# A four-layer fp32 transformer kernel: the MLA mixer's attention as a row pipeline over head pairs, and two reorderings in the last mixer

## The reference

```python
def _mla_mixer(x, w_in, g_q, g_kv, w_uq, w_ukv, w_o):
    h = x @ w_in
    c_q, c_kv, k_rope = jnp.split(h, [MLA_Q_RANK, MLA_Q_RANK + MLA_KV_RANK], axis=-1)   # 384, 256, 64
    c_q = _rmsnorm(c_q, g_q)
    c_kv = _rmsnorm(c_kv, g_kv)
    q = (c_q @ w_uq).reshape(b, s, MLA_HEADS, MLA_NOPE + MLA_ROPE)      # 8 heads of 128 + 64
    kv = (c_kv @ w_ukv).reshape(b, s, MLA_HEADS, MLA_NOPE + MLA_V)      # 8 heads of 128 + 128
    q_rope = _apply_rope(q_rope, cos[:, None, :], sin[:, None, :])
    k_rope = _apply_rope(k_rope, cos, sin)
    # blocks of 128 queries; chunk-causal mask; softmax over the keys; p @ v
    return o @ w_o

def odd_mixer(x, w_in, forget_b, dw_w, dw_b, cn_g, cn_b, w_out):
    p = x @ w_in
    y_c = forgetting_attention(q, k, v, log_f).reshape(bsz, s, D_C)     # 8 heads of 64
    y_d = conformer_conv(p[..., 3 * D_C + H_C:], dw_w, dw_b, cn_g, cn_b)
    return jnp.concatenate([y_c, y_d], axis=-1) @ w_out
```

## Time and profile before

| | |
|---|---|
| median of 3 runs | 2426.18 us (2425.48 to 2428.16) |
| the profiled execution | 2430.45 us |
| its span in the profile | 2428.7 us |
| TensorE busy | 2341.0 us, 96% |
| DVE, ACT, Pool busy | 753.6, 664.3, 1056.1 us |
| DMA | 213.91 MB, 88 GB/s |

### The profile page before, as it was taken

The page is one execution under the profiler, slowest core; times in us unless marked ns, Lnnn a source line. Parts: engine busy times, 40 slices in busy tenths (PEclk is TensorE's granted clock), DMA queues, the critical chain, the costliest instruction groups (busy, mean ns, idle before and its releaser), DMA issues.

```text
span 2428.7 us, 24625 instructions
## 1 busy us (share of the span) xinstructions
PE 2341.0 (96%) x10347; PEld 1867.6 (77%) x10347; DVE 753.6 (31%) x1434; ACT 664.3 (27%) x889; POOL 1056.1 (43%) x369
## 2 busy tenths in 40 slices
PE   8999999999999989999999999999998998999998
PEld 6666788888777668888878878888876666888887
DVE  6565200002555550000046230010169635000003
ACT  2222322222232322212222222222243463221221
POOL 4213454454323336544445645545431224654443
PEclk9999999999999989999999999999999999999999
DMA  5103222222211113222223222222220112322221
GB/s 198 40 35 121 104 88 104 95 88 95 96 53 44 65 57 122 104 94 97 83 91 108 104 105 102 89 104 78 96 95 27 44 53 87 121 104 95 96 83 56
DMA packets 32366, 213.91 MB, mean 88 GB/s; under 512 B 3584, under 2 KB 4736, under 8 KB 9216
## 3 DMA queue, kind: packets, MB, share of 16 engines
q1 hardware_dynamic: 32256, 212.34, 24.5%
HBM read 210.23 MB, written 2.10 MB: 87 GB/s over the span
## 4 chain that ended last, share of the span: by engine, by line
PE 89%; DVE 8%; ACT 1%; issue 1%; POOL 1%; DMA 0%; SPq 0%; DVEq 0%; ACTq 0%
PE bank L891 17%; PE bank L893 17%; PE bank L892 17%; PE bank L941 9%; PE bank L943 9%; PE bank L942 9%; PE bank L922 3%; DVE bank L1872 2%; PE bank L1172 1%; PE bank L927 1%; PE bank L1074 1%; PE bank L1234 1%; PE bank L1153 1%; PE bank L1279 1%; PE bank L1232 1%
## 5 line engine op out<-in xcount | busy, mean ns | idle before, releaser
L738 POOL TENSOR_TENSOR wlo<-raw,whi 128x2048 fp32r<-128x2048 f32 (+4 forms) x184 | 848.9, 4616 | 534.8 <-ACT whi L420 534.8
L891 PE MATMUL bank<-XH,whi 128*128 128x512 f32 x1832 | 722.4, 394 | 7.3 <-POOL wlo L792 6.2
L893 PE MATMUL bank<-XH,wlo 128*128 128x512 f32 x1832 | 714.9, 390 | 0.0
L892 PE MATMUL bank<-XL,whi 128*128 128x512 f32 x1832 | 714.7, 390 | 0.0
L420 ACT CAST whi<-raw 128x2048 fp32r<-128x2048 f32 (+4 forms) x184 | 350.6, 1909 | 410.3 <-PE bank L941 300.6
L891 PEld LDWEIGHTS bank<-XH,whi 128*128 128x128 f32 x1832 | 344.8, 188 | 97.4 <-issue 20.6
L893 PEld LDWEIGHTS bank<-XH,wlo 128*128 128x128 f32 x1832 | 344.7, 188 | 73.0
L892 PEld LDWEIGHTS bank<-XL,whi 128*128 128x128 f32 x1832 | 345.0, 188 | 69.6
L1571 DVE TENSOR_TENSOR hf<-sil,bank 128x512 f32<-128x512 f32 x88 | 60.5, 687 | 902.4 <-PE bank L893 855.1
L752 POOL TENSOR_TENSOR HL<-hf,HH 128x512 fp32r<-128x512 f32 x88 | 113.9, 1295 | 399.4 <-ACT HH L458 399.4
L941 PE MATMUL bank<-whi,HH 128*128 128x512 f32 x704 | 274.4, 390 | 0.0
(11 more groups left out here) (247 smaller groups left out, 2187.2 us busy)
## 6 DMA issues: line engine op xcount, KB each, us to landing
raw<-w_ffn_gu SPq DMA_DIRECT2D x88, 1024.0 KB, 4.7
raw<-w_ffn_dn SPq DMA_DIRECT2D x40, 1024.0 KB, 4.7
raw<-w_diff_in SPq DMA_DIRECT2D x7, 1536.0 KB, 6.5
GB<-gb SPq DMA_DIRECT2D x8, 1024.0 KB, 7.3
raw<-w_ev_in SPq DMA_DIRECT2D x6, 1024.0 KB, 4.8
raw<-w_od_in SPq DMA_DIRECT2D x4, 1536.0 KB, 6.6
raw<-w_mla_pair SPq DMA_DIRECT2D x4, 1280.0 KB, 6.3
raw<-w_mla_o SPq DMA_DIRECT2D x4, 1024.0 KB, 5.8
```

What stands on the lines that cost most here:

```text
L738: pool.tensor_tensor(wlo[:, off:off + size], raw[:, off:off + size], whi[:, off:off + size].bitcast(F32), ALU.subtract).then_inc(lo_ready, 1)
L891: release(pe.matmul(out, whi[:, off:off + P], xh, start=start, stop=False))
L892: pe.matmul(out, whi[:, off:off + P], xl, start=False, stop=False)
L893: return pe.matmul(out, wlo[:, off:off + P], xh, start=False, stop=stop)
```

## The change

**MLA.** The unit of swapped columns goes, in mla_in and in each pair (a pair's unit falls from 2560 to 2176 columns, eight tiles to seven). Rotation is made from one tile: DVE multiplies each quarter of 32 partitions by the sine and writes it to its neighbouring quarter, four operations, then one with the cosine and the sum. The latents' order is turned: key-value latents and the rotary key in unit 0, query latents in unit 1; pair 0's first eight steps (key and value tiles) come between the latents' groups. The loop is the odd mixer's: s = 0 to 15, both heads per step, normalisation and copies of transposes by ACT, p @ v of the pair before at qb = 1. Outputs are split from PSUM: ACT copies the bank to `XH`, DVE subtracts to `XL`; Pool has no part in it. `mVT` lies now over X, and a second probability buffer `mPT1` over the norm's parameters `GB`, so X is loaded when pair 3 begins and the first `GB` after the last output is split. `out_pair` replaces `out_units` for this mixer.

**Odd mixer.** The diagonals 20 to 30 are written ahead of `keep_conv(1)`. Outputs of pairs 0 and 1 are split from PSUM into `fYH` and `fYL`. ACT splits the last weight units at s = 12 and 14 instead of 13 and 15; its casts of k = 4, 5 come at the end of s = 12 instead of its beginning.

```diff
-STREAM = [("mla_in", (3072, 3072, 1024)), ("mla_pair", (2560,) * 4), ...
+STREAM = [("mla_in", (3072, 3072)), ("mla_pair", (2176,) * 4), ...
-PLACED = {("mla_o", 1): 2048, ("diff_in0", 1): 1536}
+PLACED = {("ffn0_gu", 1): 0, ("diff_in0", 1): 1536}
-MLA_K = (3, 3, 3, 3, 2, 2, 2, 2)
+MLA_K = (2, 2, 2, 2, 3, 3, 3)
+MLA_STEPS = [(t, k) for t in range(7) for k in range(MLA_K[t])]
+MLA_SLOTS = (MLA_STEPS[0:3], MLA_STEPS[3:5], MLA_STEPS[5:8], MLA_STEPS[8:9], MLA_STEPS[9:12], MLA_STEPS[12:13], MLA_STEPS[13:17], [])
@@ SP
-                if norm:
-                    sp.wait_ge(xn_ready, 8 * norm)
+                sp.wait_ge(*((xn_ready, 8 * norm) if norm else (va_free, 16)))
-                if u == 9:
-                    sp.wait_ge(w_used, 7)
+                if u == FIRST_UNIT["mla_o"] + 2:
+                    sp.wait_ge(w_used, FIRST_UNIT["mla_o"])
                     for t in range(NB):
                         sp.dma_start(X[:, t, :], x[t]).then_inc(x_in, 16)
@@ ACT, MLA
+            def mla_high(p):
+                for m in range(2):
+                    vax.add()
+                    act.wait_ge(va_done, vax.at())
+                    act.copy(XH[:, 2 * p + m, :], bank[6 + m][:]).then_inc(oh_ready, 1)
+            for s in range(17):
+                p, qb = divmod(s, 4)
+                if s < 16:
+                    for m in range(2):
+                        exp_row(...)
+                    sums_inverted()
+                    for m in range(2):
+                        scale_row(...)
+                if qb == 0 and s < 16:
+                    vax.add(2)
+                if qb == 1 and p:
+                    mla_high(p - 1)
+                for m in range(2) if s else ():
+                    keep_p(mPT[m], 6 + m, (s - 1) % 4)
+                if qb == 1 and p < 3 or s in (12, 13):
+                    split_w()
+            mla_high(3)
             split_w(2)
@@ ACT, odd mixer
             sigmoid(2)
+            diagonals(range(20, TAPS))
             keep_conv(1, conv_done, 1)
-            diagonals(range(20, TAPS))
             keep_conv(0, dg_used, TAPS)
...
-                if s == 12:
-                    act.wait_ge(tile_free, tiles.at())
-                    act.wait_ge(va_free, lows)
-                    for k in (0, 1):
-                        act.copy(XH[:, k, :], fY[:, k, :]).then_inc(act_hi, 1)
-                    for k in (4, 5):
-                        split_at(XH[:, k, :], fC[:, k - 4, :], swished, k - 3)
...
-                if qb == 1 or s == 15:
+                if qb == 1 and p < 3 or s in (12, 14):
                     split_w()
-                if s == 13:
-                    for k in (6, 7):
+                if s == 12:
+                    act.wait_ge(tile_free, tiles.at())
+                if s in (12, 13):
+                    for k in ((4, 5), (6, 7))[s - 12]:
                         split_at(XH[:, k, :], fC[:, k - 4, :], swished, k - 3)
@@ TensorE, MLA
+            off = begin_unit()
+            pe.wait_ge(latent_lo, 2)
+            mla_steps(off, MLA_STEPS[0:5])
+            mean_squares(5, sq[1], QR)
+            mla_steps(off, MLA_STEPS[5:8])
             spread_root(6)
+            for k in range(3):
+                pe.wait_ge(latent_lo, 3 + k)
+                mla_steps(off, MLA_STEPS[8 + k:9 + k])
+            mla_steps(off, MLA_STEPS[11:])
+            for s in range(16):
+                ...
+                for m in range(2):
+                    claim(4 + m)
+                    pe.matmul(bank[4 + m][:, 0:n], mQN[i][m][:, qb * P:n], mKN[i][m][:, 0:n], start=True, stop=False)
+                ...
+                if qb == 1 and p:
+                    mla_attend(p - 1)
+                if p < 3:
+                    mla_steps(off, MLA_SLOTS[2 * qb])
+                else:
+                    mla_out((0, 2, 4, 5)[qb])
+                for m in range(2) if s else ():
+                    p_transposes(6 + m, mL[(s - 1) % 2][m], (s - 1) % 4 + 1)
+                if p < 3:
+                    mla_steps(off, MLA_SLOTS[2 * qb + 1])
+                elif qb < 2:
+                    mla_out((1, 3)[qb])
+            for m in range(2):
+                p_transposes(6 + m, mL[1][m], NB)
+            mla_attend(3)
+            out_pair(OUT_KS, attended, (mla_late,))      # mla_late: mla_out(6), mla_out(7)
@@ DVE
+            def rope(dst, b):
+                dve.wait_ge(tile_done, tiles.at(1))
+                for q in range(4):
+                    a, o = 32 * q, 32 * (q ^ 1)
+                    dve.tensor_tensor(shift[o:o + 32, :], bank[b][a:a + 32, :], sinT[a:a + 32, :], ALU.mult).then_inc(step, 1)
+                    steps.add()
+                take(lambda: dve.tensor_tensor(dst[:], bank[b][:], cosT, ALU.mult))
+                dve.wait_ge(step, steps.at())
+                dve.wait_ge(tile_free, tiles.at())
+                dve.tensor_tensor(dst[:], dst[:], shift[:], ALU.add).then_inc(rope_ready, 1)
+            latent_tile(3, 0, sq[0], True, False)
+            latent_tile(4, 1, sq[0], False, True)
+            rope(KR, 2)
+            mean_square_root(5, RMS_EPS)
+            from_pe()
+            latents((3, 4), 7)
+            low_latents((3, 4))
+            for j in range(3):
+                latent_tile(j, (3, 0, 1)[j], sq[1], j == 0, j == 2)
+            mean_square_root(5, RMS_EPS)
+            from_pe()
+            latents((0, 1, 2), 6)
+            low_latents((0, 1, 2))
...
-                if qb == 1 and 0 < p < 3:
-                    take_value(lambda: dve.tensor_copy(fY[:, p - 1, :], bank[6][:]))
+                if qb == 1 and p in (1, 2):
+                    ohs.add()
+                    dve.wait_ge(oh_ready, ohs.at())
+                    take_value(lambda: dve.tensor_tensor(fYL[:, p - 1, :], bank[6][:], fYH[:, p - 1, :].bitcast(F32), ALU.subtract))
```

More of the change, by code:

```diff
@@ L181, in build @@
         CL = sb("CL", [P, 5, S], F32R, idle)
+        mVT = [sb(f"mVT{m}", [P, S], F32, idle) for m in range(2)]
         idle.close()
@@ L185, in build @@
         fPT1 = sb("fPT1", [P, NB, S], F32, idle)
+        idle.close()
+        idle = ExitStack()
+        mPT1 = sb("mPT1", [P, NB, S], F32, idle)
         idle.close()
@@ L1195, in _ @@
                 tile((3, 0, 1)[t], [off + (k * 3 + t) * P for k in range(KD)])
+                if t == 0:
+                    mean_squares(5, sq[0], KVR)
                 if t == 1:
-                    mean_squares(5, sq[1], QR)
-            spread_root(6)
-            mean_squares(5, sq[0], KVR)
-            off = begin_unit()
-            claim(2)
-            for k in range(KD):
-                if k == KD // 2:
-                    spread_root(7)
-                ins = product(bank[2][:], off + k * P, XH[:, k, :], XL[:, k, :], k == 0, k == KD - 1)
@@ new lines, in _, with mla_offset, mla_steps @@
+                    spread_root(7)
+            def mla_offset(t, k):
+                return (k * 4 + t) * P if t < 4 else 8 * P + (k * 3 + t - 4) * P
+            def mla_steps(off, slot):
+                steps(off, slot, MLA_K, mla_offset, CH, CL, (2, 3, 0, 1, 2, 3, 0), (3, 3, 3, 3, 0, 0, 0))
+            off = begin_unit()
[3 more added lines that the diff above has]
+            mla_steps(off, MLA_STEPS[5:8])
+            spread_root(6)
@@ L1258, in _, with mla_late @@
-                value_product(ML, mV[i][1], slice(0, P), slice(0, P), 1 if p < 3 else 0)
-            out_steps(off, OUT_MLA[-1])
-            out_units()
+                    mla_steps(off, MLA_SLOTS[2 * qb + 1])
+                elif qb < 2:
+                    mla_out((1, 3)[qb])
+            for m in range(2):
+                p_transposes(6 + m, mL[1][m], NB)
+            mla_attend(3)
+            def mla_late():
+                mla_out(6)
+                mla_out(7)
+            out_pair(OUT_KS, attended, (mla_late,))
@@ new lines, in _ @@
+            for t in range(7):
+                mla_tile(0, t)
+            for s in range(17):
+                p, qb = divmod(s, 4)
+                i, c = p % 2, 2 * (s % 2)
+                for m in range(2) if s < 16 else ():
+                    n = (qb + 1) * P
+                    row_logits(mL[s % 2][m][:, 0:n], 4 + m, n, maskT, MLA_SCALE, negmax[:, c + m:c + m + 1])
+                for m in range(2) if qb == 0 and p < 4 else ():
+                    take_value(lambda: dve.tensor_copy(mV[i][m][:].rearrange("p k d -> p (k d)"), bank[6 + m][:]))
+                if s < 16:
+                    inverse_sums(c)
+                if qb == 1 and p or s == 16:
+                    for m in range(2):
+                        low_value(2 * (p - 1) + m, 6 + m)
+                for t in finished(MLA_SLOTS[2 * qb] + MLA_SLOTS[2 * qb + 1], MLA_K) if p < 3 else ():
+                    mla_tile((p + 1) % 2, t)
```

260 lines of the change are left out of this document (82 added, 178 removed).

## The result

The changed kernel takes 2384.73 us (median of 4 runs, 2384.01 to 2388.51), the kernel before 2426.11 on the same chip: a ratio of 0.9831, 95% interval 0.9814 to 0.9848, 41.4 us less. I had forecast 24.9 us by the profile and 2401 as the median, with 2392 to 2413 as the range. It is faster, as forecast, but by more than the range allows. The profiled execution took 2385.15 (span 2383.4), so by profiled executions the gain is 45.3; the kernel before had been profiled in an execution 4.3 above its median, the changed one in one 0.4 above.

The account below looks back on a forecast made before the run. TensorE, busy 96% of the span, was taken as the bound. 13.6 - 1.9 + 7.2 - 1.5 + 3.5 + 4.0 = 24.9 us off 2430.45 gave 2405.5, and 4.3 less for the median gave 2401, range 2392 to 2413.

Parts of the forecast that it names:

- Matmuls that go: TensorE, mla_in and the MLA pairs: 60 matmuls of 128x512 fall away at 0.2267 us each, 13.6 us gained.
- Ahead of the loop: Before the MLA row loop: start at 66.1 against 71.68, 5.6 us sooner, of which 7.5 are matmuls, so -1.9 alone.
- In the loop: MLA row loop: of 11.3 us of waits and slow clock 4.1 stay, +7.2; -1.5 for unforeseen waits.
- the new stall at the first transposes: First transposes of the normalised rows: only 12 matmuls separate token block 0's halves, a wait of 2.1 us.
- the 1.5 held back for unforeseen waits: MLA row loop: 1.5 us taken off, as the odd mixer's like rows show small waits and 0.97 of clock.
- The norm's parameters: Loaded behind the last output split, 7.3 us to land, wanted by DVE some 14 us after the last attention product: 0.
- Diagonals: Odd mixer, diagonals ahead of the copies: the 9.04 us wait goes, but only DVE's idle 3.46 comes out, +3.5.
- odd outputs: Odd mixer, outputs split from PSUM: the 3.47 us wait for XL goes, ACT is late next; +4.0, between 2.3 and 7.1.
- both gaps whole: Rival, chance 0.10: both odd-mixer gaps come out whole, 11.4 instead of 3.5 and 7.1 instead of 4; 36 us, 2390.
- nothing in the odd mixer: Rival, chance 0.10: the odd mixer's edits change nothing, waits move to fK and ACT's copies; 17.4 us, 2409.
- the loss to ScalarE's chain: Rival, chance 0.15: only the matmuls count, loop waits return as waits for ACT's longer chain; 17.5 us, 2409 to 2415.
- the slow clock: Rival, chance 0.03: slower, TensorE falls to its low clock level in the row loop; 2427 or more.

Follow-up runs that it names:

- same rows: The changed kernel with both heads' rotary logit matmuls reading the same 64 partitions, order, shapes and count kept: 2395.19 us, ratio 0.9879 to the kernel before.
- head order: The changed kernel with each head's rotary matmul directly behind its own main logit matmul: 2401.12 us, ratio 0.9906 to the kernel before.

## Why the prediction was wrong, step by step

- **Matmuls that go (13.6).** Right: 60 records fewer, and putting them back costs 13.0.
- **Ahead of the loop (5.6).** Right throughout: the wait is 4.65 (5), for the mKN copy that was named; three subtractions take 1.89 (2.1); each of the four operations on 32 partitions takes 2.84 / 4 = 0.71 (0.69, not a quarter of it); 40.3 us from unit 1 to the loop against 40.5.
- **In the loop (point 3, -1.5 and +7.2).** This step failed: 147.07 us against 165.7. It took off matmuls, waits and clock, and kept for all other work the price of the kernel before, though the order of the logits' matmuls was in the diff. 11.6 of the 18.6 are the rotary part: 4 pairs at 2.91, of which same rows shows 2.14 as two matmuls at once, and the rest as order. Another 6.0 are the small differences in the pair's other rows: in the three pairs with products for a next one 15.39 - 12.36 less nine matmuls at 0.2267, which is 1.0 each (0.37 of it waits); and in all four 0.28 for the main parts, 0.28 for the transposes and 0.19 for p @ v. That these are the fewer changes from one kind of matmul to another (a row step has one group of each where two heads had two) was argued from the rows and only shown for the main parts and the rotary ones, by head order; no run isolates the 3.0 at the products, the transposes or p @ v. The last 1.0 is the balance of waits: the new stall at the first transposes is 0.70 and not 2.1, and the 1.5 held back for unforeseen waits wasn't needed, while 2.1 of smaller gaps, which I had counted as waits, are partly those same changes of kind. The norm's parameters, put at 0, cost nothing: no wait of VectorE's around the first transposes names them.
- **What I could have read.** The trace before had it, in the odd mixer that I used as the model for everything else. On TensorE's timeline there, both heads' 64-row logits of the same width:

```profile
1910.38 1.13 PE L1428 MATMUL bank<-fK,fQ 64*128 64x512 f32 x4
```

Four records, 1.06 us to the next start (1911.44), where the MLA mixer's two took 1.05. The Trainium skill, TensorE: Matmul & The Clock Gate, Part 3: Packing small matmuls, says the same: matmuls with a short contraction, whose operands start on partitions of different row groups, run concurrently. By that rule the rotary part would about halve, an estimate of 2.9 from the 5.87 a pair, 11.7 for four. The traces agree in kind and nearly in size, with 5.10 against 2.96 a pair. Had I followed it, my sum would have had all of the 11.6 that the rotary part gave, 8.6 (4 * 2.14) of them for the reason that the rule gives.
- **Diagonals (3.5) and odd outputs (4.0).** Right, at 3.4 and 4.2, and for the reasons given: VectorE's taps are back to back (18.96 for 24), the fK wait is 9.87 (about 10), the wait for fPT 2.31 (about 2). Of the rivals, both gaps whole and nothing in the odd mixer are refuted by these waits, the loss to ScalarE's chain by waits below 1 us in the loop, and the slow clock by 1.00 there.
- **From profile to median.** 4.3 was taken off for the distance of the one profiled execution from its median; the changed kernel's is 0.4. So 20.4 us of error in the profiled time became 16.3 in the median.

## What to carry to other kernels

When a change regroups work, price the new neighbours too: divide one steady period by kinds of instruction, and look for the same grouping elsewhere in the trace. A wait that goes is worth what its next one in line leaves, so write down the queue behind it (taps, then split, then GpSimd) before taking it for gained. A short multiplication on a queue that others depend on costs what stands behind it, not its own length.

## What the runs showed of the hardware

- Two fp32 matmuls of 64 rows on opposite halves of the partitions, back to back and into different banks, take 1.06 us together for 512 columns; on the same half 1.91, and with another kind between them 1.06 each.
- A VectorE multiplication by a per-row scalar in SBUF (384 columns, 2.41 us) didn't end before GpSimd's subtraction had; the next one of the same size took 0.41.
- VectorE from PSUM takes 0.71 us for 512 columns on 32 partitions, as on 128 (0.69).
- The same work behind a wait took 15.96 us at a granted clock of 1.00 and 18.84 at 0.83.
